# One-hot products per expert, router products with the weights at rest, other counts of filler matmuls, and squares of x tile by tile

## The reference

```
x = x + W_out( sig(g_r) * P_r(RG-LRU branch) + sig(g_m) * P_m(mLSTM branch) )   on rmsnorm(x)
x = x + hier_moe(rmsnorm(x))        then a final rmsnorm

g_idx  = argmax(xf @ w_rg + b_rg)                 # 1 of 4 groups
top_v, top_i = top_k(e_logits of that group, 2)   # 2 of its 4 experts
gates  = one_hot(expert) * softmax(top_v) * p(group)
for e in 16 experts:
    hdn = silu(xf @ w_g[e]) * (xf @ w_u[e])       # 2048 -> 512
    out = out + gates[:, e:e+1] * (hdn @ w_d[e])  # 512 -> 2048
```

## Time and profile before

| | us |
|---|---|
| median of 3 runs (1995.9 to 1998.81) | 1998.38 |
| the profiled execution | 2001.61 |
| its span, first to last instruction | 2000.1 |
| PE busy in the span | 1879.3 (94%) |
| DVE busy | 1241.1 (62%) |
| ACT busy | 1005.1 (50%) |
| first product begins | 27.66 |
| last product with `w_out` ends, about | 1378 |
| one-hot products begin | 1399.79 |
| ACT begins the second unit of expert weights | 1419.02 |
| last matmul, about | 1955 |

### The profile page before, as it was taken

The page is one execution under the profiler, slowest core; times in us unless marked ns, Lnnn a source line. Parts: engine busy times, 40 slices in busy tenths (PEclk is TensorE's granted clock), DMA queues, the critical chain, the costliest instruction groups (busy, mean ns, idle before and its releaser), DMA issues.

```text
span 2000.1 us, 28137 instructions
## 1 busy us (share of the span) xinstructions
PE 1879.3 (94%) x11723; PEld 1679.6 (84%) x11723; DVE 1241.1 (62%) x1437; ACT 1005.1 (50%) x999; POOL 100.9 (5%) x188
## 2 busy tenths in 40 slices
PE   6999999999999999999999999999988989898981
PEld 5999999999999999999999999998666666666650
DVE  4764634547645445664343445444799999999984
ACT  5333644653334433453334333333678787878761
POOL 3001011000000000000000000000100000000001
PEclk8999999999999999999999999999999999999996
DMA  6555554545444444445565675546599999999975
GB/s 165 160 155 139 148 143 126 144 128 146 121 123 132 118 133 132 122 119 166 150 166 150 171 194 159 157 127 240 230 375 421 399 411 398 419 394 410 402 305 157
DMA packets 379167, 422.83 MB, mean 211 GB/s; under 512 B 13823, under 2 KB 358747, under 8 KB 362969
## 3 DMA queue, kind: packets, MB, share of 16 engines
q1 hardware_dynamic: 369849, 385.55, 59.0%
q0 software_dynamic: 7504, 29.75, 4.2%
q10 hardware_dynamic: 1712, 6.04, 1.0%
HBM read 405.87 MB, written 15.45 MB: 211 GB/s over the span
## 4 chain that ended last, share of the span: by engine, by line
PE 79%; DMA 10%; DVE 5%; issue 3%; ACT 3%; ACTq 0%; POOL 0%; DVEq 0%; POOLq 0%; SPq 0%
PE bank L629 17%; PE bank L631 16%; PE bank L630 16%; DMA ring<-in_w_exp_gate 5%; DMA ring<-in_w_exp_down 4%; PE bank L931 3%; PE bank L932 3%; PE bank L933 3%; PE bank L685 3%; PE bank L789 2%; PE bank L791 2%; PE bank L790 2%; ACT w_high L1237 1%; DVE w_low L1788 1%; PE bank L737 1%
## 5 line engine op out<-in xcount | busy, mean ns | idle before, releaser
L1375 DVE TENSOR_TENSOR low<-ring,high 128x2048 fp32r<-128x2048 f32 x172 | 394.1, 2291 | 566.0 <-ACT high L1011 565.7
L629 PE MATMUL bank<-x_high,high 128*128 128x304 f32 x2160 | 662.6, 307 | 0.0
L631 PE MATMUL bank<-x_high,low 128*128 128x304 f32 x2160 | 652.0, 302 | 0.0
L1011 ACT ACTIVATE high<-ring 128x2048 fp32r<-128x2048 f32 x172 | 329.1, 1913 | 533.5 <-DMA ring<-in_w_in 317.8
L630 PE MATMUL bank<-x_low,high 128*128 128x304 f32 x1904 | 572.1, 300 | 0.0
L1788 DVE TENSOR_TENSOR w_low<-ring,w_high 128x2048 fp32r<-128x2048 f32 x192 | 430.8, 2284 | 22.2 <-ACT w_high L1237 21.4
L1237 ACT ACTIVATE w_high<-ring 128x2048 fp32r<-128x2048 f32 x192 | 363.3, 1922 | 98.0 <-DMA ring<-in_w_exp_gate 33.5
L629 PEld LDWEIGHTS bank<-x_high,high 128*128 128x128 f32 x2160 | 405.9, 188 | 5.0 <-issue 3.3
L631 PEld LDWEIGHTS bank<-x_high,low 128*128 128x128 f32 x2160 | 406.1, 188 | 0.0
L630 PEld LDWEIGHTS bank<-x_low,high 128*128 128x128 f32 x1904 | 358.5, 188 | 1.4
L904 PE MATMUL bank<-w_high,xs 128*128 128x512 f32 x512 | 210.5, 411 | 28.1 <-DVE xs L1799 12.4
(11 more groups left out here) (372 smaller groups left out, 2145.3 us busy)
## 6 DMA issues: line engine op xcount, KB each, us to landing
ring<-in_w_in SPq DMA_DIRECT2D x120, 1024.0 KB, 5.6
ring<-in_w_exp_gate SPq DMA_DIRECT2D x32, 2048.0 KB, 9.2
ring<-in_w_exp_up SPq DMA_DIRECT2D x32, 2048.0 KB, 10.9
ring<-in_w_exp_down SPq DMA_DIRECT2D x32, 2048.0 KB, 11.0
ring<-in_w_proj_rnn SPq DMA_DIRECT2D x20, 1024.0 KB, 6.1
ring<-in_w_proj_mlstm SPq DMA_DIRECT2D x16, 1024.0 KB, 6.1
ring<-in_w_out SPq DMA_DIRECT2D x16, 1024.0 KB, 6.1
slot_out<-HB POOLq DMA_DIRECT2D x16, 512.0 KB, 8.4
```

The lines of the kernel that those rows point to most:

```text
L629: pe.matmul(dst, hi[:, k, :], rhs_high(k), start=(k == 0), stop=False)
L631: last = pe.matmul(dst, lo[:, k, :], rhs_high(k), start=False, stop=(k == KD - 1))
L1011: act.activation(high[n % 4], raw[n % 4], ACT.Copy).then_inc(t_split, 1)
L1375: v.tensor_tensor(low[n % 4], raw[n % 4], high[n % 4].bitcast(F32), ALU.subtract).then_inc(t_rest, 1)
```

## The change

- **Squares as each tile lands.** `x_loaded` becomes three semaphores, one for each tile; ACT waits for the tile that it squares. A Sqrt on a spare column goes ahead of the squares. SP waits for all three as before.
- **Fillers.** `WARM` falls from 24 to 8, and `KEEP` = 2, 2, 6 fillers follow the turns of the three tiles. In the routing `keep_warm(16)` becomes 23 and the last `keep_warm(12)` becomes 17.
- **Router products.** `wrt` (20 columns) is the weight and all 304 tokens of a chunk are moved: one matmul a chunk. The result has the logits in rows; after the last chunk DVE copies them (`lt_rows`), PE turns them into tokens (three turns, waits `lt_ready`), and `logits` is signalled then.
- **Squares of the rows.** The last two groups are 12 to 14 and 15, not 12 to 13 and 14 to 15; both stand behind the loop.
- **Routing chain.** `gkey` and `ex` are computed after `chosen`; rank and count have a semaphore each (`rank_mm`, `count_mm`); the eight steps for the rounds of the slots become five.
- **One-hot products per expert.** `first_tokens(e)` runs the 48 matmuls with the 64 columns of one expert; the second expert's pass stands behind the first unit's `gate_up`. `rows_t_done` is signalled at the end of the second.

The diff (declarations of semaphores and lines that don't change are left out):

```
...
-        SQ_GROUPS = [(0, 4), (4, 8), (8, 12), (12, 14), (14, 16)]
+        SQ_GROUPS = [(0, 4), (4, 8), (8, 12), (12, 15), (15, 16)]
...
+        lt_rows = AB[:, :, :].rearrange("p a b -> p (a b)")[:, 0:T]
...
-        WARM = 24
+        WARM, KEEP = 8, (2, 2, 6)
...
-        x_loaded = sem("x_loaded")
+        x_loaded = [sem(f"x_loaded{i}") for i in range(3)]
+        X_PARTS = (2, 1, 2)
...
-            sp.wait_ge(x_loaded, 16 * 5)
+            for i in range(3):
+                sp.wait_ge(x_loaded[i], 16 * X_PARTS[i])
...
+                for _ in range(KEEP[i]):
+                    pe.matmul(bank[0][:, 0:P], ones[:, :], before[:, :], start=True, stop=True)
             pe.wait_ge(t_rest, 1)
             for k in range(KD):
                 pe.wait_ge(xnt_ready, k + 1)
...
-                for a in (0, 2, 1):
-                    t, n = TT[a]
-                    last = pe.matmul(bank[6][0:n, a * R:(a + 1) * R], x2t[i % 4][:, t:t + n], wrt[:, i, :],
-                                     start=(i == 0 and a == 0), stop=(i == KD - 1 and a == 1))
+                last = pe.matmul(bank[6][0:R, 0:T], wrt[:, i, :], x2t[i % 4][:, 0:T], start=(i == 0), stop=(i == KD - 1))
...
-                    last.then_inc(logits, 1)
+                    last.then_inc(logits_t, 1)
...
+            pe.wait_ge(lt_ready, 1)
+            for a, (t, n) in enumerate(TT):
+                last = pe.transpose(bank[5][0:n, a * R:(a + 1) * R], lt_rows[0:R, t:t + n], ident[0:R, 0:R])
+            last.then_inc(logits, 1)
             keep_warm(12)
             pe.wait_ge(var2, 1)
-            keep_warm(16)
+            keep_warm(23)
...
-                    pe.matmul(bank[5][0:n, i * NE:(i + 1) * NE], (before if j == i else ones)[0:m, 0:n],
-                              picked[0:m, j, :], start=(j == 0), stop=(j == i))
+                    last = pe.matmul(bank[7][0:n, i * NE:(i + 1) * NE], (before if j == i else ones)[0:m, 0:n],
+                                     picked[0:m, j, :], start=(j == 0), stop=(j == i))
+            last.then_inc(rank_mm, 1)
             for j, (_, m) in enumerate(TT):
                 last = pe.matmul(bank[6][:, 0:NE], ones[0:m, :], picked[0:m, j, :], start=(j == 0), stop=(j == 2))
-            last.then_inc(rank_mm, 1)
-            keep_warm(12)
+            last.then_inc(count_mm, 1)
+            keep_warm(17)
+
+            def first_tokens(e):
+
+                for k in range(KD):
+                    c = k % 4 * P + e * CAP
+                    for i, (t, n) in enumerate(TT):
+                        last = pe.matmul(bank[k // 4][:, c:c + CAP], xntok[0:n, i, k * P:(k + 1) * P],
+                                         oh[0:n, i, e * CAP:(e + 1) * CAP], start=(i == 0), stop=(i == 2))
+                    if k % 4 == 3:
+                        last.then_inc(rows_t_done if e == 1 and k == KD - 1 else first_rows, 1)
...
-            for k in range(KD):
-                for i, (t, n) in enumerate(TT):
-                    last = pe.matmul(bank[k // 4][:, k % 4 * P:(k % 4 + 1) * P], xntok[0:n, i, k * P:(k + 1) * P],
-                                     oh[0:n, i, :], start=(i == 0), stop=(i == 2))
-                if k % 4 == 3:
-                    last.then_inc(first_rows if k < KD - 1 else rows_t_done, 1)
+            first_tokens(0)
             pe.wait_ge(add2_ready, 1)
...
+            first_tokens(1)
...
-                act.dma_start(xtok[0:NM, 0, :], A["meta_tokens"]).then_inc(done, 16)
+                act.dma_start(xtok[0:NM, 0, :], A["meta_tokens"]).then_inc(done[0], 16)
...
-                    act.dma_start(xtok[p0:p0 + n, i, :], A["x_prompt"][0, r:r + n, :]).then_inc(done, 16)
-                act.dma_start(xtok[PL:NL, 2, :], A["x_sample"][0]).then_inc(done, 16)
+                    act.dma_start(xtok[p0:p0 + n, i, :], A["x_prompt"][0, r:r + n, :]).then_inc(done[i], 16)
+                act.dma_start(xtok[PL:NL, 2, :], A["x_sample"][0]).then_inc(done[2], 16)
...
-            act.wait_ge(x_loaded, 16 * 5)
...
+            act.activation(small[:, 18:19], small[:, 18:19], ACT.Sqrt)
...
+                act.wait_ge(x_loaded[i], 16 * X_PARTS[i])
...
-            squares_of_rows(len(SQ_GROUPS) - 1)
+            for g in range(len(SQ_GROUPS) - 2, len(SQ_GROUPS)):
+                squares_of_rows(g)
...
-                    if p1 is None:
-                        act.wait_ge(first_rows if b < 3 else rows_t_done, b + 1 if b < 3 else 1)
+                    if p1 is None and e == 1 and b == 3:
+                        act.wait_ge(rows_t_done, 1)
+                    elif p1 is None:
+                        act.wait_ge(first_rows, 4 * e + b + 1)
...
+            v.wait_ge(logits_t, 1)
+            v.tensor_copy(lt_rows[0:NG + NE], bank[6][0:NG + NE, 0:T]).then_inc(lt_ready, 1)
...
-                v.scalar_tensor_tensor(out=gl[0:n, i, :], in0=bank[6][0:n, i * R:i * R + NG], scalar=r_, in1=brt[0:n, 0:NG],
+                v.scalar_tensor_tensor(out=gl[0:n, i, :], in0=bank[5][0:n, i * R:i * R + NG], scalar=r_, in1=brt[0:n, 0:NG],
...
-                last = v.scalar_tensor_tensor(out=el[0:n, i, :], in0=bank[6][0:n, i * R + NG:(i + 1) * R], scalar=r_, in1=brt[0:n, NG:R],
+                last = v.scalar_tensor_tensor(out=el[0:n, i, :], in0=bank[5][0:n, i * R + NG:(i + 1) * R], scalar=r_, in1=brt[0:n, NG:R],
...
-            step(v.tensor_tensor(gkey, gl, wide_(gmx, NG), ALU.subtract))
...
-            v.tensor_tensor(ex, v2, v1, ALU.subtract).then_inc(cols_e, 1)
...
+            v.tensor_tensor(gkey, gl, wide_(gmx, NG), ALU.subtract)
+            v.tensor_tensor(ex, v2, v1, ALU.subtract).then_inc(cols_e, 1)
...
-                last = v.tensor_copy(rk[0:n, i, :], bank[5][0:n, i * NE:(i + 1) * NE])
+                last = v.tensor_copy(rk[0:n, i, :], bank[7][0:n, i * NE:(i + 1) * NE])
...
-            for m in range(1, MAXR):
-                step(v.tensor_scalar(slt, rk, float(m * CAP), float(ROUND_ROWS - CAP), ALU.is_ge, ALU.mult))
-                step(v.tensor_tensor(sl, sl, slt, ALU.add))
+            step(v.tensor_scalar(slt, rk, float(CAP), None, ALU.is_ge))
+            for m in range(2, MAXR):
+                step(v.scalar_tensor_tensor(out=slt, in0=rk, scalar=float(m * CAP), in1=slt, op0=ALU.is_ge, op1=ALU.add))
+            step(v.scalar_tensor_tensor(out=sl, in0=slt, scalar=float(ROUND_ROWS - CAP), in1=sl, op0=ALU.mult, op1=ALU.add))
...
+            v.wait_ge(count_mm, 1)
...
```

More of the change, by code:

```diff
@@ L376, in build @@
         oh_ready = sem("oh_ready")
+        logits_t = sem("logits_t")
+        lt_ready = sem("lt_ready")
+        count_mm = sem("count_mm")
         rstd_ready = sem("rstd_ready")
```

## The result

The changed kernel takes 2019.07 (median of four runs, 2015.75 to 2022.88), beside 1998.6 for the kernel before on the same chip (four runs): a ratio of 1.0093, 95% interval 1.0061 to 1.0125. It is slower by 20.5, and above the range of the prediction. The profiled execution took 2022.88 for a span of 2021.4, so 21.3 more span than before.

A forecast was written before the change was run, and what follows sets the result against it. PE was taken to bound the kernel from 45 to 1380 us, DVE and DMA to be nearly full from 1430. Start -11, router products -3.7, routing -0.2, one-hot passes +16.4 gave +1.5: 1999.9, range 1992.5 to 2008.5.

The forecast's parts named there:

- the one-hot term: Two 64-column passes of 15.2 each delay ACT's second split: 35.6 after the first pass begins, not 19.2; 16.4 lost (14.8 to 19.8).
- the four cases: Forecast's outcomes: full clock and passes of 15 (0.57), clock falls in first product (0.25), passes at floor (0.12), squares not earlier (0.06).
- case 2: Clock falls in the first product, from mixed turns and products or a short PE wait: start gains 4, 2007; chance 0.25.
- Start: Earlier squares and new fillers: first product 3.9 earlier, full clock through it, second product at 35.9; 11 gained.
- Router products: One matmul a chunk in the output stage saves about 0.25 a step; 3.7 gained (3.0 to 4.5).
- Routing: Shorter chain up to the one-hot products, against a PE pause that halves the clock: 0.2 gained (2.2 gained to 1.5 lost).
- nothing behind catches up: In the last stage, from 1430 on, a delay ahead shifts the stage as a whole.
- Case 3: One-hot passes run at the floor of weight loading, row changes hidden: 11.3 each, loss 8.6, 1992; chance 0.12.
- Case 4: Squares don't start earlier because tiles land together; PE pauses and the clock falls as before: about +11, 2010; chance 0.06.

The follow-up runs named there:

- experiment 1: Changed kernel with the single one-hot pass of 128 columns of the kernel before, all other edits kept: 1984.07, ratio 0.9932 to the kernel before.
- experiment 2: Changed kernel with its two one-hot passes, each moving all 128 columns in place of 64: 2005.92, ratio 1.0037 to the kernel before.
- experiment 4: Changed kernel with one 128-column pass in turned order (per bank, four chunks of one token tile before the next tile): 1980.6, ratio 0.9913; once more 1980.05.
- experiment 5: Changed kernel with its two passes of 64 columns, each in the turned order (per bank, four chunks of one token tile before the next): 2011.14, ratio 1.005.
- the rest alone: Changed kernel with the old start and the single 128-column pass, leaving the router products and routing chain: 1996.11, ratio 0.9986 to the kernel before.
- experiment 6: Here: changed kernel with the single 128-column pass, without the 2, 2 and 6 fillers between the start's turns: 1986.69, ratio 0.9942; runs 1984.43, 1984.44, 1988.94, 1989.34.
- experiment 7: Changed kernel with the single turned-order pass: 8 routing fillers moved ahead of the wait for copied logits, 4 dropped: 1977.63; or 12 of 35 dropped: 1979.16.

## Why the prediction was wrong

**The step that failed** is the one-hot term, and in it one silent assumption: 15.2 a pass, at the full clock. For that clock it was right: until the clock fell, a chunk of three tiles took 0.95 by the starts of the single records, which makes 15.2 a pass (15.5 by the 3.9 of the first 24 records, in which the latency is counted). At 1.2 GHz 24 records take 6.64, and a pass came to 22.9 and 22.1 by the chain of waits (start, length, what):

```profile
1387.31 22.92 PE bank L891 x96
1410.23 0.98 issue
...
1417.33 22.12 PE bank L891 x96
1439.75 1.91 ACT w_high L1255
```

The sum of the forecast to ACT's second split was 15.2 + 1.0 + 3.8 + 15.2 + 0.4 = 35.6. Measured: 22.9 + 1.0 + 6.1 + 22.1 + 0.3 = 52.4. So 16.8 were missing: 7.7 and 6.9 in the passes, 2.3 in the products between them, which ran at 0.59. The term lost 33 and not 16.4. None of the four cases had the clock fall here; the second one looked for it in the first product alone. The bounds of the term came from rows of before that were taken at or near the full clock, so both ends carried the same assumption.

**The rest of the miss** (12.5 ahead of the passes, not 14.9) is small and has four parts. *Start*: -11.1 to -11.3 in the trace, forecast -11; right at both products, and case 2 is refuted by the 1.00 in 18 to 60. The squares began at 7.77, 11.56 and 13.60, each about 1 later than forecast (tile 1 landed at 11.56 and not at 10.6); that cost nothing at the first product, which began as soon as PE was through its fillers, at 23.64 (forecast 23.8). *On the way*: one new wait on the chain, for a weight load that came late, ahead of the products with `ym_high` (waits of PE from 30 to 1400 us: total, times, longest; the first is the copied logits):

```profile
PE bank L868 <- DVE AB L1735: 1.7, 1, 1.7
PE bank L635 <- DVE low L1395: 1.6, 1, 1.6
```

The traces of experiments 1, 2, 4 and 5 and of the rest alone do not have it, so it need not belong to the change. *Router products*: 1.8 in all and not 3.7. From the router product to the turns it took 0.62 where it had taken 0.77, and the turns behind it 0.31 and not 0.28, so a step saves 0.12; the forecast had taken 0.51 for the product, from a stream of four without a change of rows. PE's timeline of the changed kernel:

```profile
1350.56 0.69 PE L843 MATMUL bank<-AB,wrt 128*20 128x304 f32 x2
1351.18 0.55 PE L849 MATMUL bank<-ident,AB 128*128 128x128 f32 x3
1351.49 0.38 PE L635 MATMUL bank<-x_high,high 128*128 128x304 f32 x1
```

*Routing*: by difference, what is left of the 12.5 (11.1 - 1.6 + 1.8 from the other three), about 1.2 gained; forecast 0.2, with bounds from 2.2 gained to 1.5 lost. The pause ahead of the logits did halve the clock for a while (70 fillers in 9.60, forecast 8.0 and 2.2 more), as assumed.

**What held.** That the upper buffers of `w_high` make ACT wait for both passes; that nothing behind catches up; that at the full clock half the columns hardly shorten a pass (15.2 to 16.95); that the three tiles of a chunk begin 0.25, 0.31 and 0.34 apart, 0.90 in sum (0.27, 0.32 and 0.36, 0.95, by the starts of the single records before the clock fell). Case 3's price, 11.3 a pass, is nearly reached by 128 columns in the turned order (12.31), but not by the change. Case 4 is refuted by the gain at the first product.

The Trainium skill (TensorE: Matmul & The Clock Gate, HAM oscillation) tells of the clock falling where PE stands idle between bursts, waiting for a transfer. The pause of 1.73 in the routing is an idle stretch too, though PE waited there for DVE. The passes are not: PE was busy for 19.00 of 19.00 us at 0.53. By what the same page of the Trainium skill says of turns (Part 4: PE-mode transpose), that they don't count as work the way products do, the second case of the forecast would have come; in the changed kernel and in the traced run without fillers the first product ran at 1.00.

Two things remain open. One is why a long stream of 64 columns lowers the clock and one of 128 does not: experiment 2 shows that the columns decide, but no count between the two was run. The other is why the clock fell behind a pause of 2.10 at the start before, and not behind one of 2.04 in the traced run of experiment 6. Other things there differ too (24 fillers and further short pauses among the turns), no run separates them, and by the two pairs of its runs that start may go either way.

## What to carry to other kernels

Before a matmul is cut into narrower ones, ask for both prices: a narrow one may cost as much as a wide one (0.11 a record here with 64 and with 128 columns, where the rows stay), and in a long stream of them the granted clock may fall although PE is "busy" in each moment; price such a term at 1.2 GHz too and let the range hold it. A delay is best followed to the one instruction that the last stage hangs on (here ACT's second split): in 13 traces what followed it took 577 to 584, while it moved over 55 us. One undivided pass, ordered by the rows of its weights, with the rest of the change gave a version that beats both kernels (1980, 0.9 to 1.0% below before).

## What the runs showed of the hardware

- One stream of fp32 records with 64 columns and weights of 128 and 48 rows was granted 2.4 GHz for its first 5 to 6 us and 1.2 GHz from then on, in three kernels and two orders; with 128 columns (experiments 1, 2 and 4) it kept 2.4 GHz, and a 64-column record in the old order went from 0.16 to 0.28 us on average when the clock fell.
- Switching between weights of 128 and of 48 rows cost 0.19 us with 128 columns moved, spread over two records (0.20 and 0.21 where others lie 0.11 apart); 24 fewer of these changes made the pass of 16.95 shorter by 4.6.
- PE's pauses don't sort by length: behind 1.73 (L868, with 0.80 shortly ahead of it) and behind 0.69 (experiment 7, with 1.15 some 6 us ahead) the clock fell, behind 1.15 there and behind 2.04 in the traced start of experiment 6 it did not.
